# The column scales of the second norm: four slabs accumulated by VectorE instead of TensorE

## The reference, cut to what matters

```python
cond = jax.nn.silu(c)
mod = cond @ w_ada[l] + b_ada[l]                # (1, 1024) @ (1024, 6144)
sh1, sc1, g1, sh2, sc2, g2 = jnp.split(mod, 6, axis=-1)
...                                             # attention gives "mixed"
x = x + g1[:, None, :] * (mixed @ w_out[l])
h2 = _rms(x, g) * (1.0 + sc2) + sh2             # the second norm
y = (jax.nn.silu(h2 @ w_gate[l]) * (h2 @ w_up[l])) @ w_down[l]
```

## Time and profile before

| | us |
|---|---|
| median of 3 runs (lowest to highest) | 778.4 (778.22 to 778.54) |
| the profiled execution, its own time | 778.42 |
| its span, first to last instruction | 776.5 |
| TensorE busy | 763.2 (98%) |
| VectorE busy | 469.4 (60%) |
| ScalarE busy | 394.2 (51%) |

### The profile page before, as it was taken

The page is one execution under the profiler, slowest core; times in us unless marked ns, Lnnn a source line. Parts: engine busy times, 40 slices in busy tenths (PEclk is TensorE's granted clock), DMA queues, the critical chain, the costliest instruction groups (busy, mean ns, idle before and its releaser), DMA issues.

```text
span 776.5 us, 10503 instructions
## 1 busy us (share of the span) xinstructions
PE 763.2 (98%) x4073; PEld 618.5 (80%) x4073; DVE 469.4 (60%) x616; ACT 394.2 (51%) x562; POOL 64.7 (8%) x84
## 2 busy tenths in 40 slices
PE   8999999999999999999999999999999999999996
PEld 6668766878888898888788877777898888888885
DVE  4667676687776564636774435447568776445355
ACT  3457877454343442535534456665455545334363
POOL 2114121000000000002440000000010000000011
PEclk9999999999999999999999999999999999999999
DMA  9999478818675457567487536316475655563601
GB/s 293 338 352 346 170 300 316 323 55 319 225 255 175 151 203 249 183 195 251 159 299 246 180 109 203 122 56 199 127 230 165 202 176 188 192 200 125 217 27 55
DMA packets 91024, 158.71 MB, mean 204 GB/s; under 512 B 3319, under 2 KB 34259, under 8 KB 89952
## 3 DMA queue, kind: packets, MB, share of 16 engines
q1 hardware_dynamic: 88336, 151.04, 58.4%
q0 software_dynamic: 2352, 6.91, 2.8%
q10 hardware_dynamic: 288, 0.10, 0.1%
HBM read 156.95 MB, written 1.08 MB: 204 GB/s over the span
## 4 chain that ended last, share of the span: by engine, by line
PE 93%; DMA 2%; SPq 2%; DVE 1%; issue 1%; ACT 0%; POOLq 0%; POOL 0%; ACTq 0%; DVEq 0%
PE PS L1057 23%; PE PS L1059 23%; PE PS L1058 23%; PE PS L1069 6%; PE PS L1070 3%; DMA raw<-in_w_ada 2%; PE PS L1308 2%; PE PS L1268 2%; SPq L962 2%; PE PS L1337 1%; PE PS L1363 1%; PE PS L1214 1%; PE PS L1079 1%; PE PS L1078 1%; PE PS L1080 1%; PE PS L1293 1%
## 5 line engine op out<-in xcount | busy, mean ns | idle before, releaser
L1706 DVE TENSOR_TENSOR wlo<-raw,whi 128x2048 fp32r<-128x2048 f32 (+1 forms) x116 | 265.5, 2292 | 147.4 <-ACT whi L1454 130.9
L1454 ACT ACTIVATE whi<-raw 128x2048 fp32r<-128x2048 f32 (+3 forms) x124 | 226.0, 1823 | 159.2 <-PE PS L1059 155.6
L1057 PE MATMUL PS<-whi,hT 128*128 128x512 f32 (+1 forms) x568 | 223.0, 393 | 0.9 <-issue 0.5
L1059 PE MATMUL PS<-whi,hT 128*128 128x512 f32 (+1 forms) x568 | 216.7, 382 | 0.0
L1058 PE MATMUL PS<-wlo,hT 128*128 128x512 f32 (+1 forms) x568 | 216.4, 381 | 0.0
L1057 PEld LDWEIGHTS PS<-whi,hT 128*128 128x128 f32 x568 | 106.9, 188 | 25.0 <-issue 5.4
L1059 PEld LDWEIGHTS PS<-whi,hT 128*128 128x128 f32 x568 | 106.8, 188 | 21.1
L1058 PEld LDWEIGHTS PS<-wlo,hT 128*128 128x128 f32 x568 | 107.0, 188 | 18.3
L1057 PE MATMUL PS<-whi,hidT 128*128 128x512 f32 x216 | 84.4, 391 | 0.0
L1059 PE MATMUL PS<-whi,hidT 128*128 128x512 f32 x216 | 84.1, 389 | 0.0
L1058 PE MATMUL PS<-wlo,hidT 128*128 128x512 f32 x216 | 84.1, 389 | 0.0
(11 more groups left out here) (275 smaller groups left out, 830.3 us busy)
## 6 DMA issues: line engine op xcount, KB each, us to landing
raw<-in_w_in SPq DMA_DIRECT2D x34, 1024.0 KB, 5.3
raw<-in_w_ff SPq DMA_DIRECT2D x32, 1024.0 KB, 5.2
raw<-in_w_ada SPq DMA_DIRECT2D x16, 1024.0 KB, 6.6
raw<-in_w_gate SPq DMA_DIRECT2D x10, 1024.0 KB, 5.7
raw<-in_w_up SPq DMA_DIRECT2D x10, 1024.0 KB, 5.3
raw<-in_w_down SPq DMA_DIRECT2D x10, 1024.0 KB, 5.3
raw<-in_w_ada SPq DMA_DIRECT2D x16, 512.0 KB, 8.5
raw<-in_w_out SPq DMA_DIRECT2D x8, 1024.0 KB, 6.2
```

Source lines behind the costliest of these rows:

```text
L1057: pe.matmul(o, ah, wh, start=(k == 0), stop=False)
L1059: return pe.matmul(o, al, wh, start=False, stop=end)
L1454: act.activation(split_view(whi, i)[:, c], slab_view(raw, slot, i)[:, c], ACT.Copy).then_inc(hi_made if i else part_whi, 1)
L1706: dve.tensor_tensor(split_view(wlo, i)[:, c], slab_view(raw, slot, i)[:, c], whole(split_view(whi, i))[:, c], ALU.subtract).then_inc(lo_ma ...
```

## The change

The four slabs of sc2 are no longer multiplied by TensorE. VectorE accumulates them in halves of 128x1024, items `scale2:m.0` and `scale2:m.1`, in a free part of `tok1` (`scale2`). Then `scale2sum` on TensorE sums over the partitions with four matmuls of 32x256; the column used is `expo`, which holds -0.5, so VectorE multiplies by -2 when it adds the bias. The slot of the ring is now given back by `scale2_used` (VectorE after the second half) where it was `ada_used` (TensorE). The order of the transfers is the same. The tables are laid out anew between `scores:7` and the norm.

```diff
-    ada = [("ada", j) for j in range(KC, 2 * KC + KC // 2)]
+    ada = [("ada", j) for j in range(KC, 2 * KC)] + [("scale2", (m, 0)) for m in range(KC // 2)]
...
 PE_ORDER
-values:4 w_out0.0 scores:6 w_out0.1 probsT:5.0 heads:7 w_out0.2 values:5 w_out0.3 scores:7 ada:16 ada:17
-probsT:6.0 w_out1.0 values:6 w_out1.1 probsT:7.0 w_out1.2 values:7 turn:diff.0.0 ada:18 ada:19 w_out1.3
-turn:diff.0.1 mod:1 w_out0.4 w_out0.5 mod:2 w_out0.6 w_out0.7 w_out1.4 turn:norm.1.0 turn:norm.1.1 turn:norm.1.2
+w_out0.3 scores:7 probsT:6.0 turn:diff.0.0 w_out1.0 values:6 probsT:7.0 w_out1.1 values:7 w_out1.2 w_out1.3
+w_out0.4 w_out0.5 turn:diff.0.1 mod:1 w_out0.6 w_out0.7 scale2sum:0 w_out1.4 mod:2 turn:norm.1.0
...
@@ SyncE: when the slot is free
+                    elif kind == "scale2":
+                        sp.wait_ge(scale2_used, i[0] + 1)
...
@@ TensorE
-                    else:
-                        k0 = 2 * (i - 2 * KC)
-                        for k in range(2):
-                            for j in range(4):
-                                c = k * D + j * 256
-                                last = pe.matmul(PS[32 * j:32 * j + 32, 7, 0:256], cond32[:, k0 + k, :],
-                                                 raw[:, slot, c:c + 256], start=first and k == 0, stop=end and k == 1)
+                elif kind == "scale2sum":
+                    take(7)
+                    pe.wait_ge(scale2_used, KC // 2)
+                    for j in range(4):
+                        last = pe.matmul(PS[32 * j:32 * j + 32, 7, 0:256], expo[:, 0:1].to_broadcast([P, 32]),
+                                         scale2[:, j * 256:(j + 1) * 256], start=True, stop=True)
+                    last.then_inc(scale2_ps, 1)
+                    reader[7] = [(mod_in, 2)]
...
@@ VectorE
+                elif kind == "scale2":
+                    m, half = i
+                    slot = landed(dve, ("scale2", (m, 0)))
+                    w, scalar = raw[:, slot, half * D:(half + 1) * D], cond32[:, 2 * m + half, 0:1]
+                    if i == (0, 0):
+                        dve.wait_ge(value_ps, FOX_P)
+                        then(dve.tensor_scalar(scale2, w, scalar, None, ALU.mult))
+                    else:
+                        last = dve.scalar_tensor_tensor(out=scale2, in0=w, scalar=scalar, in1=scale2, op0=ALU.mult, op1=ALU.add)
+                        if half:
+                            last.then_inc(scale2_used, 1)
+                            dve.wait_ge(scale2_used, m + 1)
+                        else:
+                            then(last)
+                elif kind == "scale2sum":
+                    dve.wait_ge(scale2_ps, 1)
+                    dve.scalar_tensor_tensor(out=mod[:, 2, 0:256], in0=PS[:, 7, 0:256], scalar=-2.0, in1=mod[:, 2, 0:256],
+                                             op0=ALU.mult, op1=ALU.add).then_inc(mod_in, 1)
```

More of the change, by code:

```diff
@@ L144, in fill @@
                 out.append(it)
-                n -= it[0] in ("piece", "ada")
-            while filler and filler[0][0] not in ("piece", "ada"):
+                n -= it[0] in ("piece", "ada", "scale2")
+            while filler and filler[0][0] not in ("piece", "ada", "scale2"):
                 out.append(filler.pop(0))
@@ L221, in plan @@
     order += attention(list(range(FOX_P + DIFF_P)), tail, ada[11:12])
+    order += [("scale2", (m, 1)) for m in range(KC // 2)] + [("scale2sum", 0)]
     order += turns("diff", 0, (1,)) + insert(slab(wo[0], "w_out", 0, 4), (2, [("mod", 1)])) + [("evac", wo[0])]
@@ L345 @@
[L345 to L354, removed]
@@ new lines @@
+ada:14 ada:15 probsT:4.0 heads:6 values:4 w_out0.0 scores:6 w_out0.1 probsT:5.0 heads:7 w_out0.2 values:5
+w_out0.3 scores:7 probsT:6.0 turn:diff.0.0 w_out1.0 values:6 probsT:7.0 w_out1.1 values:7 w_out1.2 w_out1.3
+w_out0.4 w_out0.5 turn:diff.0.1 mod:1 w_out0.6 w_out0.7 scale2sum:0 w_out1.4 mod:2 turn:norm.1.0
+turn:norm.1.1 turn:norm.1.2 turn:norm.1.3 norm:1 gate0.0 gate0.1 gate0.2 gate0.3 gate0.4 gate0.5 gate0.6
+gate0.7 up0.0 up0.1 up0.2 up0.3 up0.4 up0.5 up0.6 up0.7 gate1.0 gate1.1 gate1.2 gate1.3 turn:hid.0.0
@@ L364 @@
[L364 to L378, removed]
+EV:diff0 probsT:0.0 probsT:0.1 heads:2 values:0 lam:0 scores:1 split:13 probsT:1.0 heads:3 scores:2
@@ new lines @@
+probsT:1.1 EV:diff1 values:1 split:14 scores:3 probsT:2.0 probsT:2.1 heads:4 values:2 split:15 scores:4
+probsT:3.0 probsT:3.1 heads:5 values:3 EV:diff2 scores:5 probsT:4.0 heads:6 values:4 split:16 scores:6
+probsT:5.0 heads:7 values:5 scores:7 probsT:6.0 split:17 values:6 turn:diff.0.0 probsT:7.0 values:7
+turn:diff.0.1 split:18 sums:1.0 split:19 sums:1.1 part:norm.1.0 part:norm.1.1 split:20 part:norm.1.2
+part:norm.1.3 split:21 EV:gate0 split:22 split:23 split:24 turn:hid.0.0 turn:hid.0.1 split:25 EV:gate1
@@ L379 @@
+scores:12 probsT:12.0 probsT:12.1 heads:14 values:12 scores:13 EV:gb0 split:80 probsT:13.0 probsT:13.1
+heads:15 values:13 scores:14 split:81 probsT:14.0 probsT:14.1 scores:15 values:14 split:82 EV:ga1
+turn:merge.0.0 turn:merge.0.1 split:83 probsT:15.0 probsT:15.1 split:84 EV:gb1 values:15 turn:merge.1.0
+split:85 turn:merge.1.1 split:86 split:87 turn:norm.3.0 sums:3.0
 """)
@@ L382 @@
 split:12 EV:diff0 lam:0 scores:2 probs:1 values:0 split:13 probs:2 EV:diff1 unit:2 scores:3 unit:3 values:1
[L383 to L391, removed]
@@ L397 @@
-turn:merge.0.0 probs:15 turn:merge.0.1 split:83 EV:ga1 split:84 back:15 merge:1 turn:merge.1.0 turn:merge.1.1
-split:85 EV:w_out20 split:86 turn:norm.3.0 turn:norm.3.1 split:87
+split:14 probs:3 scores:4 values:2 split:15 probs:4 scores:5 probs:5 values:3 ada:15 scale2:0.0 scores:6
+split:16 probs:6 scale2:0.1 scores:7 diffnorm:0 probs:7 split:17 turn:diff.0.0 scale2:1.0 scale2:1.1
+diffnorm:1 mod:1 turn:diff.0.1 scale2:2.0 split:18 scale2:2.1 scale2:3.0 scale2:3.1 EV:w_out0 scale2sum:0
+EV:w_out1 mod:2 gained:norm.1.0 gained:norm.1.1 gained:norm.1.2 part:norm.1.0 part:norm.1.1 split:19
@@ L399 @@
+split:79 back:11 probs:12 scores:13 back:12 probs:13 scores:14 split:80 scores:15 back:13 EV:ga0 split:81
+merge:0 probs:14 split:82 back:14 turn:merge.0.0 probs:15 turn:merge.0.1 split:83 EV:ga1 split:84 back:15
+merge:1 turn:merge.1.0 turn:merge.1.1 split:85 EV:w_out20 split:86 turn:norm.3.0 turn:norm.3.1 split:87
 """)
 PIECE_AT = {(p["T"], p["k"]): (p["slab"], p["off"]) for kind, p in ORDER if kind == "piece"}
-STREAM = [it for it in ORDER if it[0] in ("split", "ada", "chunk", "gate2")]
+STREAM = [it for it in ORDER if it[0] in ("split", "ada", "chunk", "gate2") or it[0] == "scale2" and not it[1][1]]
```

101 lines of the change are left out of this document (61 added, 40 removed).

## The result

| | before | changed |
|---|---|---|
| median of 5 runs (lowest to highest), us | 778.4 (777.71 to 778.6) | 787.6 (786.43 to 788.12) |
| profiled execution / its span, us | 778.42 / 776.5 | 788.12 / 786.2 |
| mean granted clock of the span | 0.998 | 0.992 |
| TensorE / VectorE busy, us | 763.2 / 469.4 | 764.4 / 479.0 |

The changed kernel is slower: ratio 1.0115, 95% interval 1.0104 to 1.0126, or 9.2 us.

The account below looks back on a forecast made before the run. TensorE, with 93% of the chain that ended last, was taken as the bound. 778.42 before, plus 5.4 from waits less saved work, plus 0.25 for `mod:2`, gave 784.1 us (own bounds 783.2 to 785.2); the range was 782.3 to 787.3.

Parts of the forecast that it names:

- the clock: Rival: TensorE's granted clock falls while it idles ahead of `scale2sum`; 785.5 to 790 us, taken as 787; chance 0.23.
- wait E: TensorE at `scale2sum` waits for VectorE's queue of halves and `split:18`; 4.7 us, bounds 4.4 and 5.2.
- A: TensorE ahead of `probsT:6.0` waits for VectorE's last read of the PSUM bank of `scores:7`; 1.37 us.
- D: TensorE ahead of `w_out0.6` waits for the result of `turn:diff.0.1`; 1.7 us, bounds 1.4 and 2.0.
- B: TensorE ahead of `turn:diff.0.0` waits for VectorE's `diffnorm:0`; 0.35 us.
- TensorE's work: Four sc2 slabs, 3.74 us, leave TensorE and `scale2sum`, about 0.5 us, comes: net 3.2 us less.
- The walk without the clock: TensorE followed through its new order from `scores:7`, at full clock: 784.1 us, bounds 783.2 to 785.2.
- wait C: TensorE ahead of `values:7` waits for ScalarE's copy to `pt`; 0.8 us, bounds 0.3 and 1.0.
- `mod:2` in the chain to `hT`: VectorE writes `AB` behind `EV:w_out1`, between the last x and `hT`; 0.25 us, bounds 0 and 0.4.
- Slots given back later: A transfer of up weights now waits for `scale2:2.1`; costs nothing, with 12 us to spare.
- Rival 2: VectorE keeps up: late halves and `split:18` do not hold `scale2sum`; 779.4 us, chance 0.04.
- rival 3: TensorE finds all operands ready and keeps the whole 3.2 us of removed work; 775.2 us, chance 0.02.

Follow-up runs that it names:

- idle matmuls in both places: Changed kernel with nine idle matmuls ahead of TensorE's wait at `scale2sum` and three ahead of that at `probsT:6.0`; 784.59 us, ratio 1.0080.
- the order with little load: Changed kernel with 64 of 1024 columns in every half but the first on VectorE, order kept; 781.88 us, ratio 1.0049.
- the removal alone: Kernel before with one matmul of eight kept in each of the four sc2 slabs, nothing added on VectorE; 777.57 us, ratio 0.9990.
- the other order: Changed kernel, same work reordered: `w_out1.0` ahead of `probsT:6.0`, six halves ahead of `split:17`, `scale2sum` behind `w_out0.5`; 778.42 us, ratio 1.0001.

## Why the prediction was wrong

The step that failed is the clock: it stood as a rival with a chance of 0.23, behind wait E alone, and the sum of the forecast had nothing for it. All five runs had a mean clock of 0.992 to 0.994 against 0.996 to 0.999 in the runs of the kernel before, and the profiled one had two low stretches. What the clock cost is 3.0 us, by idle matmuls in both places. That the rival had 3 us as well is luck: it was half of a bound for one stretch behind wait E, and that stretch cost about 2.0 in the profiled run, with 1.5 in another that the rival did not have. What misled me is the argument by one long wait. The end of the program showed a fall after about four microseconds without a matmul, and I took waits of 1.4 and 1.7 us for harmless. The profiles have falls right behind 1.5 and 0.3 us, and behind 1.8 us. A wait of that size need not bring one: the profiled runs of two experiments, idle matmuls in wait E alone and the order with little load, have waits A to D and a full clock there. But with three waits that can each bring a fall (A with B, D, and E), a fall in most runs was the likely case, and the range should have been built around it.

By the Trainium skill ("TensorE: Matmul & The Clock Gate", part 1, the section "A second HAM failure mode: psum-queue depth-cycling") very short idle times between groups of matmuls, when they come often enough, make the clock swing between its two levels. The trace agrees as far as it goes: the clock was 0.50 behind gaps of 1.5 and 0.3 us. The page gives no length for its idle times, so no run here shows that these gaps are what it means. I had weighed only the page's case of one long gap.

Point by point:

- TensorE's work, 3.2 us less: held by the distances (1.87 and 1.86 us of slabs gone, 0.57 of `scale2sum` come). TensorE's busy time did not fall by 3.2, as forecast; it rose by 1.2 in the profiled run (763.2 to 764.4), because matmuls at the low clock count longer. With the same work on TensorE and the clock full at the place (the profiled run of the order with little load) it is 760.4, 2.8 less than before.
- The walk without the clock: 784.6 against 784.1. Of the 0.5, 0.2 is `scale2sum` (0.57 and not 0.5) and the 24 matmuls behind it (5.6 and not 5.45). The whole, 783.2 to 785.2, was set narrower than the bounds of its terms add up to, about 782.6 to 785.5; 784.6 lies in both.
- Waits A to E, 8.9 us: measured 8.7, each within 0.3 of its forecast and inside its bounds. Released by what was named: the maxima, `diffnorm:0`, ScalarE's copy, `turn:diff.0.1`, the halves. One reading in wait C was off: ScalarE's start of `values:6` was not bound by `split:17` but by TensorE (0.29 us idle ahead of it at full clock, in the order with little load; 1.89 in the changed kernel's profile); the wait came out near the forecast all the same.
- `mod:2` in the chain to `hT`, 0.25 us: from the end of `w_out1.7` to `gate0.0` is 5.84 us (166.14 to 171.98) where it was 5.60 (156.70 to 162.30), 0.24 more.
- Slots given back later: nothing, as said. The 614.20 us behind `gate0.0` are the same.
- Rival 2 (VectorE keeps up) and rival 3 (all is gained): VectorE did not keep up, and the removal alone gives 0.9 us, so neither came.
- "I am wrong if the granted clock shows a stretch below 1.00 between 150 and 170": it did (155.5 to 162.4), and another before 140 that I had not named.

The 9.1 us from 778.5 to 787.6 divide by the runs: 2.5 for the order with little load at full clock (780.95; one execution, with its wait of 0.9 ahead of the sum), 3.6 for the load of the halves on top of it (784.6), 3.0 for the clock. The first two are not the order's and the load's own for good: the other order carries the full load in the time of the kernel before, so it is the two together, halves placed where TensorE waits for VectorE, that made 6 of the 9.

What stays open is which of the waits brings a fall in which run; it differs between runs of one kernel, and I did not separate what decides it.

## What to carry to other kernels

Work that looks like cost on the bounding engine may be the cover of a chain beside it: walk the engine through the new order and give each operand a time, and move work off it only together with other filler. Put work on a second engine ahead of the steps that others wait for only as far as that engine is idle there; the same eight steps cost nothing in one order and nine microseconds in another. Look at the short waits of TensorE and not only at the longest: here waits of 1.5 and 1.8 us had a low clock behind them in some runs and not in others. Give the clock a term in the sum, and test it with idle matmuls in the waits.
